# A transformer block pair on one core: parameters at the end of the weight queue, reordered mixers, and a top-k search with projection work beside its scores

## The reference, cut to what matters

```
proj = rms_norm(x) @ w_in                      # r_q r_k r_v r_g d_q (512 each), d_c, d_pe, d_g, i_q, i_k, i_w
rel = relu(einsum('bthd,bsd->bths', q_idx, k_idx) * idx_scale)     # 8 heads of 32
score = einsum('bth,bths->bts', w_idx, rel)                        # 1024 x 1024, causal by chunks of 64
top_val, top_idx = lax.top_k(score, 256)                           # per token
logits over the chosen 256 keys -> softmax -> values
```

## Time and profile before

| | us |
|---|---|
| median of 3 runs | 2377.84 (2376.99 to 2378.47) |
| the profiled execution's own time | 2380.34 |
| its span, first to last instruction | 2378.6 |
| busy: PE / DVE / ACT / POOL | 2162.4 / 1251.6 / 711.8 / 389.5 |
| mean granted TensorE clock | 0.939 |

### The profile page before, as it was taken

How to read it: one execution, slowest core, us unless ns; L and a number is a source line. 1 busy time by engine, 2 the same in 40 slices (tenths; PEclk the granted TensorE clock), 3 DMA queues, 4 the chain that set the end, 5 groups by cost and what they waited for, 6 DMA issues and landing times. The chain is left out here.

```text
span 2378.6 us, 27580 instructions
## 1 busy us (share of the span) xinstructions
PE 2162.4 (91%) x10421; PEld 1592.8 (67%) x10421; DVE 1251.6 (53%) x2244; ACT 711.8 (30%) x1250; POOL 389.5 (16%) x469
## 2 busy tenths in 40 slices
PE   4999989987997999999999997758999886999998
PEld 2854464476445888888888886626888773757876
DVE  4762694348573333223444325289999463762433
ACT  1232111021002323222444223263212243771325
POOL 0920011023000000000000000301782541300110
PEclk7999999988998999999999998768999998999999
DMA  6443120001213333234434232201111102003101
GB/s 257 167 129 122 35 71 1 0 1 72 97 54 106 97 97 97 80 97 151 124 115 118 84 97 65 63 5 27 49 49 49 40 1 79 2 1 125 71 1 71
DMA packets 185202, 176.29 MB, mean 74 GB/s; under 512 B 12726, under 2 KB 157430, under 8 KB 181770
## 3 DMA queue, kind: packets, MB, share of 16 engines
q1 hardware_dynamic: 178538, 163.89, 22.2%
q0 software_dynamic: 2880, 10.49, 1.2%
q10 hardware_dynamic: 3680, 0.54, 0.1%
HBM read 160.98 MB, written 12.60 MB: 73 GB/s over the span
## 5 line engine op out<-in xcount | busy, mean ns | idle before, releaser
L1720 DVE TENSOR_TENSOR ff_part<-ff_raw,ff_part 128x1024 fp32r<-128x1024 f32 (+2 forms) x152 | 164.9, 1085 | 433.9 <-ACT ff_part L1634 433.8
L1531 PE MATMUL ps<-h,ff_part 128*128 128x512 f32 x704 | 275.3, 391 | 4.1 <-DVE ff_part L1720 4.1
L1532 PE MATMUL ps<-h,ff_part 128*128 128x512 f32 x704 | 274.8, 390 | 0.0
L1533 PE MATMUL ps<-h,ff_part 128*128 128x512 f32 x704 | 274.6, 390 | 0.0
L1634 ACT ACTIVATE ff_part<-ff_raw 128x1024 fp32r<-128x1024 f32 (+2 forms) x152 | 144.0, 948 | 433.0 <-PE ps L1533 431.0
L1531 PE MATMUL ps<-pj_part,h 128*128 128x512 f32 (+1 forms) x448 | 174.9, 390 | 11.0 <-POOL pj_part L2148 6.8
L1532 PE MATMUL ps<-pj_part,h 128*128 128x512 f32 (+1 forms) x448 | 174.4, 389 | 0.0
L1533 PE MATMUL ps<-pj_part,h 128*128 128x512 f32 (+1 forms) x448 | 174.3, 389 | 0.0
L2207 DVE TENSOR_SCALAR_CACHE_REDUCE pj_junk<-NM,prm 128x384 uint8<-128x384 f32 (+1 forms) x186 | 163.7, 942 | 1.1
L1531 PEld LDWEIGHTS ps<-h,ff_part 128*128 128x128 f32 x704 | 132.7, 188 | 32.1 <-DVE ff_part L1720 4.5
L1533 PEld LDWEIGHTS ps<-h,ff_part 128*128 128x128 f32 x704 | 132.7, 188 | 27.7
(11 more groups left out here) (568 smaller groups left out, 3892.3 us busy)
## 6 DMA issues: line engine op xcount, KB each, us to landing
ff_raw<-in_w_ffn_in SPq DMA_DIRECT2D x88, 512.0 KB, 3.8
s_wm<-in_w_mod SPq DMA_DIRECT2D x16, 1024.0 KB, 4.8
ff_raw<-in_w_ffn_out SPq DMA_DIRECT2D x32, 384.0 KB, 3.3
pj_raw<-in_w_in SPq DMA_DIRECT2D x48, 256.0 KB, 2.6
ff_raw<-in_w_ffn_out SPq DMA_DIRECT2D x32, 320.0 KB, 3.1
mod_w<-in_w_mod SPq DMA_DIRECT2D x8, 1024.0 KB, 9.3
mod_x<-in_x SPq DMA_DIRECT2D x8, 512.0 KB, 14.8
w_out<-in_w_out SPq DMA_DIRECT2D x4, 1024.0 KB, 8.7
```

Source lines behind the costliest of these rows:

```text
L1531: nc.tensor.matmul(out, w[0], x[0], start=first, stop=False)
L1532: nc.tensor.matmul(out, w[0], x[1], start=False, stop=False)
L1533: return nc.tensor.matmul(out, w[1], x[0], start=False, stop=last)
L1720: v.tensor_tensor(part[s % 2][1][:, 0:n, :], raw[s][:, 0:n, :], part[s % 2][0][:, 0:n, :].bitcast(F32), ALU.subtract).then_inc(lo, 1)
```

## The change

It has five parts: the S5 parameters are loaded by SP behind x, and C is transposed last; in the mixers, projection groups are put into the places where PE waited, with the banks rearranged; r_q and r_k are computed in halves of four token tiles, 88 of their 128 triples before and between the scores; of each search count, the two widest tiles are only compared on DVE and summed by ACT, whose other work follows a plan made of two constants (0.68 us per triple, 4.9 us per bit); and the masks are made in the attention stage.

```diff
 # stage_modulate, SP (the same DMAs go from ACT's queue; C copy goes to the end of DVE's program)
             for i in range(tiles):
                 sp.dma_start(xr[i][:], src(i)).then_inc(x_in[i // 2], 16)
+            for a, name in enumerate(("s5_c_re", "s5_c_im")):
+                for dup in range(2):
+                    sp.dma_start(Z.Cn[:, a, :, dup, :], ...).then_inc(S["cin"], 16)
             sp.wait_ge(w_use, KT)
             sp.dma_start(Z.wd[:], ...)
+            # s5_b_re, s5_b_im, s5_d, s5_glu_b
 # PE: the block "wait cin; transposes of Cn into bank 5" moves from before the sums to behind the last x group
+            pe.wait_ge(S["cin"], 16 * 4)
+            pe.wait_ge(h_act, 4 * (NG - 1)); pe.wait_ge(h_dve, 4 * (NG - 1))
 # stage_s5: dve.wait_ge(S["bin"], 16 * 4) first, and on ACT before the last sigmoids
 # stage_mixers, PE
             n = slab(1, n, range(loads[1]))
+            n = slab(2, n, range(1))
             pe.wait_ge(S["conv"], 1)
...
-            pe.wait_ge(S["ev"], int(first[3]))
+            n = slab(2, n, range(1, loads[2]))
+            pe.wait_ge(S["ev"], int(first[3]) - 1)
...          # gate rows now in banks 0-2 and 3-5 (flatps[..., 3 * a * HALF + c * P:])
+            n = slab(3, n, range(2))
             pe.wait_ge(S["gcp"], 2)
-            n = slab(3, n, range(4))
+            n = slab(3, n, range(2, 5))
...          # bmm
-            n = slab(3, n, range(4, loads[3]))
-            pe.wait_ge(S["ev"], total)
+            n = slab(3, n, range(5, loads[3] - 1))
+            pe.wait_ge(S["ev"], total - 2)
...          # columns: K.ident[0:QS, 0:QS]
             last.then_inc(S["colmm"], 1)
+            n = slab(3, n, range(loads[3] - 1, loads[3]))
             pe.wait_ge(S["colev"], 1)
 # ACT: slab(3) range(7), then the exponentials, then the last three; row copies are one per direction
 # stage_project
+    NH, NP = NT // 2, len(slabs) + 2
+    lead, beside = 26, 88
+    wide = np.cumsum([e - c for i, c, e, m in groups])
+    quota = [lead + int((beside - lead) * x / wide[-1]) for x in wide]
+    ahead = [KT + q // NH + 2 for q in quota]
+    TRIPLE, BIT = 0.68, 4.9
+    def begins(u):       # planned start of part u on PE, 0 at triple 88
+        return TRIPLE * ((u - KT) * NH if u < 5 * KT else 4 * KT * NH + (u - 5 * KT) * NT) - TRIPLE * beside
 # PE
             slab(0)
+            queries(0, lead - 6)
             pe.wait_ge(S["ev"], NT)
             pe.wait_ge(S["rope"], 1)
+            # turn(0..3); queries(lead - 6, lead - 3); turn(4..7); queries(lead - 3, lead)
             pe.wait_ge(S["iev"], NT)
             for n, (i, c, e, m) in enumerate(groups):
-                if n >= 2:
-                    pe.wait_ge(S["relr"], 4 * (n - 1))
+                if n:
+                    pe.wait_ge(S["relr"], 4 * n)
                 # 4 score matmuls, now always in banks 4 to 7
                 mm.then_inc(S["smm"], 1)
+                queries(quota[n - 1] if n else lead, quota[n])
+            queries(beside, 3 * KT * NH)
             pe.wait_ge(S["relr"], len(pieces))
-            with pe.Fori(1, len(slabs)) as j:
+            queries(3 * KT * NH, 4 * KT * NH)
+            with pe.Fori(5, NP) as j:
                 slab(j)
 # ACT: between relu groups split(...) while made < ahead[n], and two half slabs are written out
+            def slab_work(made, taken, until):
+                while True:
+                    more = made < NP * KT and begins(made) - 8.0 < until
+                    done = taken < NT * (len(slabs) - 2) and ends(taken) - 1.5 < until
+                    ...  # the earlier of: split part `made`, write out tile `taken` (which waits for PE)
             act.wait_ge(S["used"], len(pieces))
+            made, taken = slab_work(made, 0, 3.0)
+            for b in range(32):
+                for j in range(NB - 2, NB):
+                    act.wait_ge(S["cmp"], 2 * b + j - (NB - 2) + 1)
+                    nc.scalar.activation(x, x, ACT.Copy, accum_out=cnt[:, j:j + 1]).then_inc(S["counted"], 1)
+                made, taken = slab_work(made, taken, 3.0 + BIT * (b + 1))
+            slab_work(made, taken, 1.0e6)
 # POOL: the 16 turns of r_q and r_k, one in each of the parts of r_v and r_g; those of d_q in the last slab
+                    if n in (5, 6):
+                        turn(n - 4, 0, FREQ_R, slice(k, k + 1))
+                    elif n == NP - 1 and k >= 4:
+                        turn(5, FREQ_R, FREQ_A, slice(2 * (k - 4), 2 * (k - 3)))
 # DVE
-            def count(bound):
-                for j in range(NB):
+            def count(bound, b):
+                for j in range(NB - 2, NB):
+                    v.tensor_scalar(junk[:, packed(j + 2)], K.NM[:, packed(j + 2)], bound(j), None, ALU.is_ge).then_inc(S["cmp"], 1)
+                for j in range(NB - 2):
                     x = K.NM[:, packed(j + 2)]
                     last = v.tensor_scalar(junk[:, packed(j + 2)], x, bound(j), 0.0, ALU.is_ge, ALU.add, accum_out=cnt[:, j:j + 1])
                 link(last)
+                dve.wait_ge(S["counted"], 2 * (b + 1))
                 link(v.tensor_scalar(keep[:], cnt[:], TOPK - 0.5, None, ALU.is_ge))
 # stage_attention: the six masks (as L2221 to L2226, in three parts each) on DVE, L2227 on ACT
+            for i in (7, 6, 5, 4):          # DVE, before its wait for the prepared keys
+                for part in range(3):
+                    mask(i, part)
+            # tiles 3 and 2: one part behind each of the steps 3, 5, 7, 9, 11, 13
+            def lower(i):                   # ACT; for 7, 6, 5, 4 before the first exponential
+                act.wait_ge(S["pick"], NT - i)
+                x = K.NM[:, packed(i)]
+                nc.scalar.activation(x, x, ACT.Copy, scale=-LOW, bias=LOW).then_inc(S["masked"], 1)
```

More of the change, by code:

```diff
@@ L346, in _ @@
                 last.then_inc(h_tr, 1)
+            pe.wait_ge(S["cin"], 16 * 4)
+            pe.wait_ge(h_act, 4 * (NG - 1))
+            pe.wait_ge(h_dve, 4 * (NG - 1))
+            for a in range(2):
+                for h in range(2):
+                    last = nc.tensor.transpose(K.bank[5][:, (2 * a + h) * P:(2 * a + h + 1) * P], Z.Cn[:, a, h, :, :], K.ident[:])
+            last.then_inc(S["part"], 1)
 def mod_bias(K, bank, g, first):
@@ L1959 @@
 PJ_KB, FREE_KB, SMALL_KB = 88, 24, 18
+NB = NT - 2
 def packed(i):
@@ L2055, in slab, with queries, turn @@
                     last.then_inc(S["um"], 1)
[L2057 to L2061, removed]
-                    pe.wait_ge(S["iev"], i - 3)
+            def queries(lo, hi):
+                for t in range(lo, hi):
+                    u, i = t // NH, t % NH
+                    half, k = u // KT, u % KT
+                    if i == 0:
+                        pe.wait_ge(S["lo"], KT + u + 1)
+                    if k == 0 and half < 3:
+                        pe.wait_ge(S["ev"], (NT + (half - 1) * NH if half else 0) + i + 1)
+                    at = (half % 2 * NH + i) * P
+                    last = product(nc, K.bank[i + (NH if half == 3 else 0)][:], [x[:, k, at:at + P] for x in K.h3], [w[:] for w in part[k % NR]], k == 0, k == KT - 1)
+                    if i == NH - 1:
+                        last.then_inc(S["um"], 1)
+                    elif k == KT - 1:
+                        last.then_inc(S["tm"], 1)
+            def turn(i):
                 b = K.bank[4 + i % 4]
@@ new lines, in slab_work @@
+            def slab_work(made, taken, until):
+                while True:
+                    more = made < NP * KT and begins(made) - 8.0 < until
+                    done = taken < NT * (len(slabs) - 2) and ends(taken) - 1.5 < until
+                    if not more and not done:
+                        return made, taken
+                    if more and (not done or begins(made) - 8.0 < ends(taken) - 1.5):
+                        split(made // KT, range(made % KT, made % KT + 1))
+                        made += 1
+                    else:
+                        take_one(taken)
+                        taken += 1
@@ L2108, in _ @@
             split(1, range(3))
-            take(0)
-            split(1, range(3, 4))
+            take_first()
+            split(1, range(3, lead // NH + 1))
             for i in range(NT):
@@ L2435, in stage_attention @@
     w_in = [K.sem(f"at_win{b}") for b in range(2)]
[L2436 removed]
+    names = "zero uk wuv spread whi wlo turn ukr latr pre prer lmm logit mx er tr pa pd pv ot back done pick masked chain".split()
     S = {n: K.sem("at_" + n) for n in names}
```

226 lines of the change are left out of this document (136 added, 90 removed).

## The result

The changed kernel takes 2343.52 us as the median of 4 executions (2338.89 to 2345.85), the kernel before 2377.41 us. The ratio is 0.9853 with a 95% interval of [0.9841, 0.9865]: 34 us faster, where 46 were forecast. The profiled execution took 2344.68 us and has a span of 2342.9.

A forecast was written before the change was run, and what follows sets the result against it. PE was taken to bound the slab projection beside the search, with DVE 25 us behind. Terms -16 - 19 - 13 + 2 = -46 gave 2332 us against the median; own range 2320 to 2345, 8-in-10 range 2304 to 2354.

The forecast's parts named there:

- the first stage: First stage: loading parameters from SP behind x and transposing C last saves 16 us, bounds -18 and -4.
- the mixers: Mixers: projection groups cover PE's waits of 6.6, 4.7, 4.0 and 2.2 us; -19 us, bounds -20 and -14.
- the search stage: Search stage: -38 us if PE never waits, +25 for late parts; -13 in all, bounds -38 and +6.
- rival 3: First stage: SP's added load issues hold the first barrier up to 12 us later; 2344 us, chance 0.10.
- rival 2: Search stage: DVE and POOL exclude each other fully, scores +22 us, PE 34 us late; 2347 us, chance 0.14.
- the transposes of C wait for all eight: First stage: C's transposes wait for eight parameter DMAs, though C is only half; ending at 44 to 45, not 61.0.
- Search stage, its beginning: Before and during scores: first sum 6.3 us later, POOL contention adds 16.3; -38 us if PE never waits.
- the rule that the prediction named: Scores: the Trainium skill says VectorE and GpSimd lock each other out for whole instructions; contention 22 us rather than 16.3.
- I take the middle, 26, less 1: Search bits: PE's lateness from POOL lengthening bits, between 16 and 35 us, less the plan's lead; +25 us.
- Rival 1: Search bits: comparisons find POOL idle, bits stay near 4.9 us, PE is not late; 2307 us, chance 0.25.
- Rival 4: Search: ACT, DVE and PE lock step, adding 48 us; mean bit 7.1 us, total 2395 us, chance 0.03.
- Attention: Attention stage: masks moved here are mostly covered by DVE's idle time; +2 us, bounds 0 and +5.

The follow-up runs named there:

- explate: Changed kernel with the mixers' exponentials again after all write-outs of slab 3 and the last projection group before the column matmuls: 2353.46 us (single execution).
- dvecounts: Changed kernel with all six counts and their sums back on DVE, none on ACT, which hands out splits without waiting for the search: 2307.47 us.

## Why the prediction was right in the sum and wrong in a part

Taken stage by stage, three of the four terms fell outside their own bounds: the first stage (-18.5, bounds -18 and -4), the mixers (-26.2, bounds -20 and -14) and the search stage (+6.9, bounds -38 and +6). The errors cancelled in part. The measured 2343.5 us is nearer to the number of rival 3 (2344), whose mechanism did not happen, and of rival 2 (2347) than to the 2332 of the forecast.

**First stage, right for the wrong reason.** -16 forecast, -18.5 measured; SP's last load was issued at 41.02 and the stage ended at 42.52, so rival 3 didn't happen: the added issues on SP took 4.96 us at most, not 16.65. (The forecast's own parts add up to an end at 45.5 and not at 44 to 45; the last tile of x was there at 37.6 rather than 39.5.) The step "the transposes of C wait for all eight" named the wait that ended last in the trace. The issue that blocks ACT's queue for 16.65 us was read as the reason of C's lateness, while it held ACT's sines and with them all of x.

**Mixers, mechanism right, size short.** All four waits went, as forecast, 18.2 us with the small one behind slab 2. The term that was missing is the clock: 26.2 - 18.2 = 8 us, which include about 1 for the narrower columns. The stage's granted clock rose from 0.94 to 0.97 and PE's busy time fell by 8.6 us. explate shows it for two of the four places: 6.9 us of waits, 4.4 more behind them.

**Search stage, its beginning: right, a little small.** First sum 70.9 us after the start of the stage, forecast 69.6. The sums took 80.4 us, forecast 76.9. Before and after, by shape:

```profile
L2196 DVE SCALAR_TENSOR_TENSOR NM<-pj_rel,prm,NM 128x512 f32<-128x512 f32 x42 | 31.6, 752 | 1.5
```

```profile
L2295 DVE SCALAR_TENSOR_TENSOR NM<-pj_rel,prm,NM 128x512 f32<-128x512 f32 x42 | 41.6, 991 | 2.0 <-ACT pj_rel L2216 0.6
```

With the narrower shapes the contention was 14.6 us, forecast 16.3. The 22 of the rule that the prediction named did not come: 16 subtractions fell into the sums and cost DVE 0.91 us each, while an undisturbed one lasts 1.28. What I had left out are 5.6 us in which DVE waited for ACT's relu, which now has splits and write-outs between; the scores now also use four banks in place of eight, and no run separates the two. The cost of PE's 62 triples there is so 19.8 us for 42.6 us of work: this part of the change is good.

**Search stage, the bits: the step that failed.** "I take the middle, 26, less 1" stood for PE's lateness of 25 us; it was 40, which is 15 of the 20 us by which the stage missed its forecast. The other 5 are the later first sum and the longer sums. Two things in the 25 were mis-sized. First, with POOL quiet a bit was to last 4.95 us and, with the plan near 4.9, to hand out parts in time; in the first bits a subtraction already met the short operations, since it comes at a fixed place in the bit, and they took 6.2 us. Second, under rotations both comparisons and two of the three short operations were met in every bit, 6.94 us, because ACT's split ties POOL's work to DVE's phase; I had priced a chance meeting (0.25 + 0.5). A third of PE's waits, 10.9 us, was for write-outs, which the forecast had not looked for. The upper bound of 35 was exceeded by 5; 8 of the 40 are slower matmuls behind the waits, which no term held. The forecast did name the mechanism and its place. Rival 1 (the plan holds) was wrong for the change; dvecounts has its time, 2307, by taking the plan away. For this stage alone rival 2, with PE 34 us late and +2, came nearer than the forecast; but it asked for 22 us of contention in the scores and over 40 us of waits, and there were 14.6 and 32. Rival 4 is out by the same 32, and by a mean bit of 6.27 us where it asked for 7.1.

**Attention.** Forecast +2, measured +0.1. DVE's first logits still come after an idle 7.61 us, behind the four wide masks; the narrow masks cost nothing visible:

```profile
1974.24 1.23 DVE L2716 CUSTOM_DVE_ANT_0 at_prob<-ps,NM 128x1024 f32<-128x1024 f32 x1 [7.61 <-PE ps L2598]
```

**Left open.** The 2.0 us by which the other stages were longer in this profile. 1.6 of them are in the stages between the mixers and the search, where no edit falls, and in other kernels of the study they were shorter again (the search stage of dvecounts began at 1456.8, that of the changed kernel at 1459.7).

## What to carry to other kernels

Before a reduction is split off to another engine to shorten an instruction, look whether the form that remains is one that a busy neighbour can hold up: here the longer instruction was immune and the shorter one not, and so sharing shortened the search by 8.4 us only, and it cost PE 40. An engine that serves two masters in one static order (here ACT, for the search and for the projection) couples them in both directions, and of three constants in its plan none did as well as untying it (2343.5, 2319.9 and 2329.0 us against 2307.5): free the server first, tune afterwards. And a removed wait of TensorE can be worth more than its length: here two waits of 6.9 us in front of small matmuls cost 11.3.

## What was not expected of the hardware

The clock's price for short waits: 40 column matmuls took 8.83 us behind a wait of 4.68 us, at half the granted clock, and 4.61 us without it. The comparison with its sum is untouched by GpSimd (means of 1275 and 1142 ns in kernels with and without POOL's rotations), while the one without rises from 0.75 to over 1 us. And `COPY_PREDICATED` of six columns, 0.17 us alone, took 1.21 us where a subtraction ran.
